# Products of constants on TensorE during three norms, and router logits interleaved with the transposes of the token rows

## The reference

```
x <- LayerNorm(ALPHA * x + Mixer(x));  x <- LayerNorm(ALPHA * x + FFN(x))

Mixer: one input projection whose columns feed
  (A) a causal pooling mixer, (B) a Conformer convolution (GLU, depthwise conv 31, LayerNorm, swish),
  (C) a Griffin recurrent branch (conv 4, RG-LRU, GeLU gate);
  three branch projections, merged by sigmoid gates, then one output projection
FFN: dense SwiGLU (2816 columns) in layer 0; in layer 1 the sum over the top 2 of 8 experts (3584 columns):
  logits = x @ router; top_vals, top_idx = top_k(logits, 2); gates = softmax(top_vals)
  y = sum_e combine[:, e] * swiglu(x, w_gate[e], w_up[e], w_down[e])
```

## Time and profile before

| | us |
|---|---|
| median of 3 runs | 1568.91 (1568.13 to 1569.36) |
| the profiled execution, its own time | 1571.72 |
| its span | 1569.9 |
| PE busy | 1425.3 (91%) |
| DVE busy | 1360.8 (87%) |
| ACT busy | 1133.5 (72%) |
| mean granted TensorE clock | 0.959 |

### The profile page before, as it was taken

The page is one execution under the profiler, slowest core; times in us unless marked ns, Lnnn a source line. Parts: engine busy times, 40 slices in busy tenths (PEclk is TensorE's granted clock), DMA queues, the critical chain, the costliest instruction groups (busy, mean ns, idle before and its releaser), DMA issues.

```text
span 1569.9 us, 40893 instructions
## 1 busy us (share of the span) xinstructions
PE 1425.3 (91%) x17657; PEld 1169.1 (74%) x17657; DVE 1360.8 (87%) x1446; ACT 1133.5 (72%) x1074; POOL 107.6 (7%) x149
## 2 busy tenths in 40 slices
PE   6999898999999979799989899999899888798786
PEld 4778687888778768698687697788777765765663
DVE  4899977546579997799999999999999999999996
ACT  3797575434458766577788878888888888888883
POOL 2121013000043001100000000000000000000001
PEclk9999899999999999799999999999999999999998
DMA  9645444546544534369999999999999999999991
GB/s 299 252 163 180 154 167 160 175 161 228 188 173 162 202 121 165 135 245 382 402 398 402 412 394 396 388 395 407 408 408 406 411 400 410 400 405 411 406 410 62
DMA packets 141203, 464.89 MB, mean 296 GB/s; under 512 B 8086, under 2 KB 10262, under 8 KB 126652
## 3 DMA queue, kind: packets, MB, share of 16 engines
q1 hardware_dynamic: 138828, 456.46, 76.3%
q0 software_dynamic: 2048, 5.55, 1.2%
q10 hardware_dynamic: 144, 0.23, 0.1%
HBM read 460.79 MB, written 2.89 MB: 295 GB/s over the span
## 4 chain that ended last, share of the span: by engine, by line
PE 36%; DVE 29%; DMA 14%; issue 13%; ACT 5%; POOL 1%; SPq 1%; DVEq 0%; ACTq 0%
PE ps L733 11%; PE ps L734 11%; PE ps L735 11%; DVE w_lo L2043 9%; DMA stage<-in_moe_w_gate 7%; DVE w_lo L2046 4%; DMA stage<-in_moe_w_up 3%; DVE w_lo L1525 3%; ACT w_hi L1461 2%; DVE arena L1650 2%; DVE arena L1639 2%; DMA stage<-in_w_in 2%; DMA stage<-in_moe_w_down 1%; DVE z L2033 1%; ACT w_hi L1167 1%
## 5 line engine op out<-in xcount | busy, mean ns | idle before, releaser
L733 PE MATMUL ps<-arena,w_hi 128*128 128x128 f16 (+7 forms) x3952 | 568.0, 214 | 19.5 <-issue 7.5
L735 PE MATMUL ps<-arena,w_lo 128*128 128x128 f16 (+7 forms) x3952 | 568.1, 214 | 13.3 <-issue 13.3
L734 PE MATMUL ps<-arena,w_hi 128*128 128x128 f16 (+7 forms) x3952 | 568.1, 214 | 11.3 <-issue 11.1
L2043 DVE SCALAR_TENSOR_TENSOR w_lo<-stage,w_hi 128x2048 f16<-128x2048 f32 x218 | 492.6, 2289 | 22.3 <-ACT w_hi L1461 21.5
L1461 ACT ACTIVATE w_hi<-stage 128x2048 f16<-128x2048 f32 x218 | 453.5, 2105 | 76.6 <-DMA stage<-in_moe_w_gate 33.7
L733 PEld LDWEIGHTS ps<-arena,w_hi 128*128 128x128 f16 x3952 | 388.0, 99 | 35.3 <-DVE w_lo L2043 14.8
L734 PEld LDWEIGHTS ps<-arena,w_hi 128*128 128x128 f16 x3952 | 388.2, 99 | 19.8 <-issue 12.3
L735 PEld LDWEIGHTS ps<-arena,w_lo 128*128 128x128 f16 x3952 | 388.2, 99 | 17.4 <-issue 12.0
L733 PE MATMUL ps<-xh,w_hi 128*128 128x264 f16 x1184 | 333.3, 282 | 29.8 <-issue 11.5
L734 PE MATMUL ps<-xl,w_hi 128*128 128x264 f16 x1184 | 332.9, 281 | 0.0
L735 PE MATMUL ps<-xh,w_lo 128*128 128x264 f16 x1184 | 332.9, 281 | 0.0
(11 more groups left out here) (311 smaller groups left out, 1203.4 us busy)
## 6 DMA issues: line engine op xcount, KB each, us to landing
stage<-in_moe_w_gate SPq DMA_DIRECT2D x112, 1024.0 KB, 9.1
stage<-in_moe_w_up SPq DMA_DIRECT2D x112, 1024.0 KB, 9.7
stage<-in_moe_w_down SPq DMA_DIRECT2D x112, 1024.0 KB, 9.7
stage<-in_w_in SPq DMA_DIRECT2D x44, 1024.0 KB, 5.8
stage<-in_ffn_w_gate SPq DMA_DIRECT2D x10, 1024.0 KB, 5.0
stage<-in_ffn_w_up SPq DMA_DIRECT2D x10, 1024.0 KB, 5.3
stage<-in_ffn_w_down SPq DMA_DIRECT2D x10, 1024.0 KB, 5.1
stage<-in_w_out SPq DMA_DIRECT2D x8, 1024.0 KB, 5.3
```

The source lines that it names most:

```text
L733: mm(out, ah, bh, start=start, stop=False, skip_group_check=True)
L734: mm(out, ah, bl, start=False, stop=False, skip_group_check=True)
L735: return mm(out, al, bh, start=False, stop=stop, skip_group_check=True)
L2043: V.scalar_tensor_tensor(paired(w_lo, n), as_loaded(stage, n), WS, paired(w_hi, n), ALU.mult, ALU.subtract).then_inc(S["lo_done"], 1)
```

## The change

`keep_busy` is new: n float16 products of 128 x 512 on constants (`ident16` is stationary, `spare_rows` are the first 256 float32 words of `consts`, read as 512 float16), written to a bank that the next real product overwrites. It is called 23 times before the first product after norm 0 and after norm 1, 21 times before the logits of norm 2, 6 times before the ranks and 4 times before the gather. After norm 2 the logits and the transposes of a channel tile now follow one another, tile after tile, and the six `empty` of the `xtok` banks stand ahead of the first tile. ACT and DVE read the `xtok` banks by half (h) first and block (i) second; the table load for the sigmoid is no longer ahead of ACT's copies; of the six `token_lo` one stands ahead of the ranks, and five behind the one-hot matrix.

```diff
@@ constants
+        spare_rows = consts[:, 0:2 * P].bitcast(F16)
+        NORM_IDLE = 23
@@ PE
+            def keep_busy(out, n):
+                for _ in range(n):
+                    mm(out, ident16[:, :], spare_rows, start=True, stop=True, skip_group_check=True)
@@ rows_half(..., idle=0): before its first product
                 if ready and half == 0:
                     steps.sort(key=lambda jk: jk[1])
+                    if idle:
+                        empty(pe, names_[0])
+                        keep_busy(bank(names_[0]), idle)
@@ first piece of layer 1, and of the dense FFN
-                                rows_half(slot, names_, half, 512, lambda kk: pe.wait_ge(S["x_split"], KT + kk + 1))
+                                rows_half(slot, names_, half, 512, lambda kk: pe.wait_ge(S["x_split"], KT + kk + 1), NORM_IDLE)
-                                              lambda kk: pe.wait_ge(S["x_split"], kk + 1))
+                                              lambda kk: pe.wait_ge(S["x_split"], kk + 1), NORM_IDLE)
@@ PE after norm 2
             empty(pe, "logits")
+            keep_busy(bank("logits"), NORM_IDLE - 2)
+            for i in range(3):
+                for h in range(2):
+                    empty(pe, ("xtok", i, h))
+
             for k in range(KT):
                 pe.wait_ge(S["norm_ready"], k + 1)
                 for i in range(3):
                     n = P if i < 2 else NS_
                     t = mm(bank("logits")[0:n, i * NE:(i + 1) * NE], x[:, k, i * P:i * P + n], w_rt[:, k, :],
                            start=(k == 0 and i == 0), stop=(k == KT - 1), skip_group_check=True)
-            t.then_inc(full_of("logits"), 1)
-            def token_rows(i):
...
-            for i in range(3):
-                token_rows(i)
+                    if k == KT - 1 and i == 2:
+                        t.then_inc(full_of("logits"), 1)
+                for i in range(3):
+                    n = P if i < 2 else NS_
+                    name = ("xtok", i, k // 4)
+                    t = nc.tensor.transpose(bank(name)[0:n, k % 4 * P:(k % 4 + 1) * P], x[:, k, i * P:i * P + n], ident)
+                    if k % 4 == 3:
+                        t.then_inc(full_of(name), 1)
+
+            empty(pe, "ranks")
+            keep_busy(bank("ranks"), 6)
             pe.wait_ge(S["tri_ready"], 2)
             pe.wait_ge(S["mask_ready"], 1)
-            empty(pe, "ranks")
...
+            empty(pe, ("gath_hi", 0))
+            keep_busy(ps[:, 6, :], 4)
             gather((0, 0), None)
@@ ACT
-            table(ACT.Sigmoid)        
-            for i in range(3):
...
+            for h in range(2):
+                for i in range(3):
...
@@ DVE
-            token_lo(0)
-            token_lo(1)
+            token_lo(0, 0)
 
             dve.wait_ge(S["mask_ready"], 1)
             filled(dve, "ranks")
...
             t.then_inc(S["onehot_ready"], 1)
+            token_lo(1, 0)
             dve.wait_ge(S["rows_zeroed"], 6)
-            token_lo(2)
+            token_lo(2, 0)
+            for i in range(3):
+                token_lo(i, 1)
```

More of the change, by code:

```diff
@@ L810, in stats, with rows_half @@
                         mm(bank(mean)[:, 0:T], ones_d[:, :], zsum, start=False, stop=False, skip_group_check=True)
-            def rows_half(slot, names_, half, width, ready=None):
+            def rows_half(slot, names_, half, width, ready=None, idle=0):
                 steps = [(j, k) for j in range(len(names_)) for k in range(4)]
@@ L1407, in _ @@
                     norm(1, ("mean", 1), 0, "ln2_g", "ln2_b")
-            table(ACT.Sigmoid)
-            for i in range(3):
[L1412 to L1415, removed]
+            for h in range(2):
+                for i in range(3):
+                    n = P if i < 2 else NS_
+                    if i == 2:
+                        act.wait_ge(S["rows_zeroed"], 6)
                     name = ("xtok", i, h)
@@ L1909, in _, with token_lo @@
             V.tensor_tensor(route1[:, 3, :], route1[:, 0, :], route1[:, 1, :], ALU.subtract).then_inc(S["gd_ready"], 1)
[L1910 to L1917, removed]
-            token_lo(0)
-            token_lo(1)
+            def token_lo(i, h):
+                name = ("xtok", i, h)
+                dve.wait_ge(S["xt_hi"], 3 * h + i + 1)
+                n = P if i < 2 else NS_
+                V.tensor_tensor(xtl[0:n, i, h * 512:(h + 1) * 512], bank(name)[0:n, :],
+                                xth[0:n, i, h * 512:(h + 1) * 512], ALU.subtract).then_inc(free_of(name), 1)
+            token_lo(0, 0)
             dve.wait_ge(S["mask_ready"], 1)
```

## The result

The changed kernel took 1575.77 us, median of 5 runs (1570.86 to 1577.85); the kernel before 1568.91, median of its 5 (1566.46 to 1573.31). The ratio is 1.0032, 95% interval 1.0018 to 1.0046: slower, as forecast (1576). The ratio on record isn't the quotient of the two medians, which is 1.0044; by it the loss is 5 us (2.8 to 7.2), by the medians 6.9. The profiled execution took 1573.62 us, its span is 1571.7.

A forecast was written before the change was run, and what follows sets the result against it. PE's idle stretches and half-clock work around the norms were taken as the bound, with shifts at the gather reaching the end. -1.35 + 0 + 8.7 = 7.3 us on 1568.91 gave 1576; own range 1573 to 1580, with rivals from 1567.5.

The forecast's parts named there:

- Norm 0: Behind norm 0, 23 constant products fit in PE's idle time and avoid the slow restart: gain 1.35 us, between 0 and 2.3.
- Norm 1: Behind norm 1, PE restarts quicker but waits longer at the pooling product, about 5 us: gain 0, between 0 and 2.3.
- The start: At norm 2, the first logits product waits for bank 0, which DVE's centring of tile 7 frees: 3.1 us later.
- The clock: In the mixture of logits and transposes, clock falls to 0.50 within 1.5 us: 1.73 us a tile, 13 to 14 us.
- The six constants: Ahead of the ranks, six constant products at 0.50 take 2.6 us, to 669.4; the ranks follow 5.3 us later than before.
- The fourth low part: Behind the one-hot matrix, the gather's first product waits for bank 6, which the fourth `token_lo` frees: 2.5 us.
- Four constants and gather: Ahead of the first expert, four constant products and the gather's 48 products take 5.6 us together, between 3.6 and 6.9.
- Sum of the routing: After norm 2, the first expert's product starts 8.7 us later, between 6.7 and 10, and the shift reaches the end.
- The whole: Over the whole kernel, -1.35 + 0 + 8.7 makes it 7.3 us slower.
- The first rival: Clock holds in the routing: eight tiles in 7.0 us, gather shifted 0 to +3 us, 1567.5 to 1570.5 us; chance 16%.
- The third rival: Clock comes back mid-routing, by the six constants or earlier, saving part of 8.7 us: 1570 to 1573 us; chance 13%.
- The second rival: Bank free in time, clock holds everywhere, norm 1's gain arrives: gather ends 2.9 us earlier, 1562.4 us or about 1564; 6%.

The follow-up runs named there:

- e4: The changed kernel without the six constant products ahead of the ranks and the four ahead of the gather; ratio 1.0030 to the kernel before.
- e3: The changed kernel with each wait for an `xtok` bank moved to the first transpose that writes into it; 1567.07 us against 1571.94, ratio 0.9975.
- e9: e3 without the four constant products ahead of the gather; ratio 0.9973 to the kernel before.
- e5: The changed kernel, early bank waits kept, with 39 constant products instead of 21 ahead of the logits; ratio 1.0036 to the kernel before.
- e1: The kernel before with only the 23 constant products at norm 0 and at norm 1, old routing; ratio 0.9968.
- e14: The same instructions as e12, run again for a second profile; ratio 1.0023 to the kernel before.
- e12: The changed kernel with late bank waits and 39 constant products instead of 21 ahead of the logits; ratio 1.0038 to the kernel before.
- e13: e9 with DVE's low parts moved: two ahead of the logits' read, two behind the mask, two behind the one-hot matrix; 1564.67 us against 1569.52, ratio 0.9973.
- e7: The kernel before with constants at all three norms and one more ahead of each tile's logits, all logits still before all transposes; ratio 0.9980.

## Why the prediction was right, point by point

The view that decided was one row of DVE against the new order on PE: the last reader of bank 0. The routing, from which the sign comes, was read rightly. That the time came out at 1575.77 against 1576 is in part luck: the profiled executions differ by 1.9 us and not by 7.3, the ratio on record gives 5, and the terms below come to 5.8.

- Norm 0: -1.35 forecast, -0.9 measured. The restart was as said, 13 products in 1.47 us, but PE then caught up with the norm and lost 0.45 us in front of DVE's last `xl`: a wait that the slow products had covered.
- Norm 1: 0 forecast, -0.3 in this trace and -1.5 on average over the traces. The gain is partly kept, by a path that I hadn't seen; the wait at the pooling product didn't grow to 5 us, it shrank to 0.9, since a wait for ACT ahead of it had grown to 2.9. Within the bounds, but a wrong mechanism.
- The start: 3.1 us later forecast, 3.3 measured (9.16 - 5.90 us behind the last sum). Right.
- The clock: right, it fell about 1 us into the logits. The mixture took 12.3 us, not 13.5: a tile at 0.50 takes 1.62, not 1.73.
- The six constants: 2.6 us of time on the path forecast. They took 2.5 on PE and cost nothing, as e4 shows. The prediction has DVE's experts at 669.0 and the constants' end at 669.4, so by its own numbers only 0.4 us were theirs. Its 5.3 us for the ranks was the distance of the right two points, so the sum stood, but the name of what costs was wrong. The ranks came 4.2 us later, 1.1 less than forecast, as the mixture was 1.2 us shorter.
- The fourth low part: 2.3 us more from the ranks to PE's next work, 2.5 forecast. Right. Four constants and gather took 6.3 us against 5.6, nearly all at half clock, within the bounds.
- Sum of the routing: 8.7 forecast, 8.2 measured. The expert stage was 1.4 us shorter in this trace, which lies within its spread over the traces (897.7 to 900.8): it gave nothing back that can be told.
- The whole: 8.2 of the routing less 0.9 and the average 1.5 of norms 0 and 1 is 5.8, where the prediction had 7.3.

The first rival, that the clock holds through the routing (16%), failed: with the wait the clock fell within 1.1 us, in three traces of three. A mixture at full or nearly full clock came only with no such idle stretch ahead of it: 7.7 us in e3 and e9, 7.8 in e5, against the 7 that the rival says. The third rival, that the clock comes back in the middle (13%), was half right: it rose again behind the six constants (1.00 in 664 to 666), but PE then did nothing but wait for DVE, and it was at 0.50 again for the gather, so nothing was saved.

The second rival, that the bank is free in time and the clock holds (6%), had the condition that e3 makes true. Its routing gained 0.56 us there and not 2.9. The mixture ends 6.2 us earlier against the last sum; the mask's chain, which the transposes used to cover (2.7), the low parts behind the one-hot matrix (2.3) and the four constants (1.7) take that back; the gather gives 1.0, of which 0.57 is the wait for DVE's count that falls away.

## What to carry to other kernels

Put a wait for a buffer directly ahead of the first instruction that writes it; taken all at once ahead of a loop it waits for the slowest reader of all, and if PE idles there, the work behind it can run at half clock as well (here 3.35 us of wait, and 5.4 more behind it). When work is interleaved, list what used to lie beside the part that vanishes: here the choice of the experts lay under the transposes and came out bare. Filling an idle stretch with products of constants paid ahead of the long float16 stages of norms 0 and 1 (ratio 0.9968); ahead of the short float32 logits no gain shows in the ratios (e3 and e9 against e1), and a longer filling lost. A single profile can't measure it, because the clock behind other idle stretches differs between executions.

## What the runs showed of the hardware that was not expected

- A stage of small float32 products need not hold the full clock even without idle time ahead of it or in it: it fell 4.3, 7.3 and 7.6 us into the mixture in e14, e12 and e5 (at most 0.14 us idle ahead), 7.6 us in e13 (0.67 idle ahead) and 4.5 us into the logits of e7; in e3 and e9 it held for the 7.7 us. The float16 products between norm 0 and norm 1 of the changed kernel kept 1.00 throughout.
- The clock can fall during an idle stretch or behind it: at norm 2 of the changed kernel it read 1.00 in the whole of 646 to 648, where PE did nothing, and fell when PE was at work again; in e1 it read 0.50 from 646 to 648, where PE did nothing either.
- The Trainium skill, page TensorE: Matmul & The Clock Gate, LDWEIGHTS, gives a weight load one price, its columns over 1.2 GHz, with no second one for the array's other clock. The traces don't agree with it for float32: the load of 128x128 took 322 ns at the low clock and 190 at the full one, and the logits of one tile with their loads took 0.64 us at full clock (e3) and 0.99 at half (e14).
- Identical instructions ahead of norm 0 took 235.70 to 240.59 us, and that went with the clock behind one idle stretch near 184 us.
- PE can stand idle for 1.7 to 2.0 us in a row of transposes with nothing that the profile shows to wait for (e5, e12, e14).
